# The lead panels of a stage take turns as the blocks of X come, the panel steps around the squares' sums are dealt out anew, and ScalarE writes two output blocks of each norm

## The reference

```python
h = _layer_norm(DEEPNORM_ALPHA * h + mix, ln_g[layer, 0], ln_b[layer, 0])
h = _layer_norm(DEEPNORM_ALPHA * h + _sq_relu_mlp(h, ffn_w1[layer], ffn_w2[layer]), ...)
# _layer_norm: mu = mean(x); var = mean((x - mu)^2); (x - mu) * rsqrt(var + eps) * g + b
```

## Time and profile before

| | us |
|---|---|
| median of 3 runs | 2793.14 |
| the profiled execution | 2793.86 |
| its span, first to last instruction | 2792.1 |
| PE busy | 2707.3 |
| DVE, ACT, POOL busy | 1281.0, 1016.3, 283.2 |
| mean granted clock of TensorE | 0.987 |

### The profile page before, as it was taken

The page is one execution under the profiler, slowest core; times in us unless marked ns, Lnnn a source line. Parts: engine busy times, 40 slices in busy tenths (PEclk is TensorE's granted clock), DMA queues, the critical chain, the costliest instruction groups (busy, mean ns, idle before and its releaser), DMA issues.

```text
span 2792.1 us, 39535 instructions
## 1 busy us (share of the span) xinstructions
PE 2707.3 (97%) x16362; PEld 2360.0 (85%) x16362; DVE 1281.0 (46%) x2178; ACT 1016.3 (36%) x1630; POOL 283.2 (10%) x357
## 2 busy tenths in 40 slices
PE   8999999999999999999999999999999999999997
PEld 7888899999988888788888888888888887888886
DVE  5544654334532323563334543435657655633333
ACT  4554443222322223352223432323567443522221
POOL 0000300001200000210000310002211121200003
PEclk9999999999999999999999999999999999999998
DMA  3111233222111212232222132222321212232220
GB/s 139 54 47 47 83 123 107 91 91 77 46 61 63 97 61 76 91 106 91 98 98 91 70 118 98 91 84 68 121 76 66 93 46 99 82 101 97 95 64 31
DMA packets 66531, 232.94 MB, mean 83 GB/s; under 512 B 8880, under 2 KB 9264, under 8 KB 65968
## 3 DMA queue, kind: packets, MB, share of 16 engines
q1 hardware_dynamic: 66352, 230.41, 24.8%
HBM read 228.25 MB, written 2.10 MB: 83 GB/s over the span
## 4 chain that ended last, share of the span: by engine, by line
PE 86%; DVE 5%; ACT 4%; POOL 2%; issue 2%; DMA 1%; SPq 0%; DVEq 0%; POOLq 0%; ACTq 0%
PE ps L578 75%; PE ps L887 2%; POOL R L2624 2%; PE ps L1013 1%; PE ps L588 1%; DVE R L1890 1%; PE ps L767 1%; PE ps L727 1%; DVE HT L1884 1%; ACT HT L1240 1%; POOL S L2610 1%; PE ps L874 1%; PE ps L598 1%; PE ps L1110 1%; PE ps L611 1%
## 5 line engine op out<-in xcount | busy, mean ns | idle before, releaser
L578 PE MATMUL ps<-XH,WH 128*128 128x264 f32 (+2 forms) x1856 | 538.3, 332 | 14.4 <-DVE XL L2584 8.6
L578 PE MATMUL ps<-XH,LENT 128*128 128x512 f32 (+2 forms) x2096 | 532.1, 343 | 8.0 <-DVE XL L1906 7.9
L578 PE MATMUL ps<-XL,WH 128*128 128x264 f32 (+2 forms) x1856 | 523.6, 324 | 0.0
L578 PE MATMUL ps<-XH,WL 128*128 128x264 f32 (+2 forms) x1856 | 522.7, 324 | 0.0
L578 PE MATMUL ps<-HH,LENT 128*128 128x264 f32 (+2 forms) x2220 | 491.1, 319 | 1.9 <-DVE LENT L1862 1.9
L1862 DVE TENSOR_TENSOR WL<-RAW,WH 128x1024 fp32r<-128x1024 f32 (+1 forms) x232 | 286.5, 1235 | 270.9 <-ACT WH L1210 270.6
L578 PEld LDWEIGHTS ps<-XH,LENT 128*128 128x128 f32 x2096 | 359.1, 190 | 60.0 <-DVE XL L1906 11.8
L578 PEld LDWEIGHTS ps<-HH,LENT 128*128 128x128 f32 x2220 | 361.4, 190 | 32.0 <-DVE LENT L1862 2.3
L578 PEld LDWEIGHTS ps<-XH,WH 128*128 128x128 f32 x1856 | 319.1, 189 | 56.7 <-issue 19.1
L578 PEld LDWEIGHTS ps<-XH,WL 128*128 128x128 f32 x1856 | 318.9, 189 | 28.1
L578 PEld LDWEIGHTS ps<-XL,WH 128*128 128x128 f32 x1856 | 319.1, 189 | 26.6
(11 more groups left out here) (215 smaller groups left out, 2625.1 us busy)
## 6 DMA issues: line engine op xcount, KB each, us to landing
RAW<-in_wf SPq DMA_DIRECT2D x128, 512.0 KB, 3.3
RAW<-in_wr SPq DMA_DIRECT2D x48, 512.0 KB, 3.3
RAW<-in_wg SPq DMA_DIRECT2D x44, 512.0 KB, 3.3
RAW<-in_wu SPq DMA_DIRECT2D x44, 512.0 KB, 3.3
RAW<-in_wd SPq DMA_DIRECT2D x32, 512.0 KB, 3.3
RAW<-in_we SPq DMA_DIRECT2D x24, 512.0 KB, 3.3
RAW<-in_wm SPq DMA_DIRECT2D x24, 512.0 KB, 3.3
RAW<-in_wro SPq DMA_DIRECT2D x16, 512.0 KB, 3.3
```

The lines of the kernel that those rows point to most:

```text
L578: mm = e.matmul(o[:, to:to + m], wt, xt[:, k, c0 + a * m:c0 + (a + 1) * m], start=(n == 0 and j == 0), stop=(n == nk - 1 and j == 2))
```

## The change

- `lead_turns` gives the order in which the lead panels take their steps. Half 0: five steps of panel 0, five of panel 1, three of each, then one panel after the other; for ln00 panels 0 to 2 by turns, with panels 3 and 4 put in. Half 1: panels 0 to 2 by turns for the eight blocks, then panel 3, then panel 4. An eviction follows its panel's eighth step. All three engines use the same order.
- `first_steps`: 12 instead of 8 steps ahead of the second total in ln00. Ahead of the squares' sums 20 instead of 17 steps, but for ln1 and mem.
- The output blocks k = 2 and 5 of every norm (not mem's) are written by ACT instead of POOL, from the same tile, behind XH of the same block; who reads them waits for `S.r_act`.
- `even`: three steps of weo 1 ahead of the turns of unit 41, two between them and the values, two behind, instead of seven ahead.
- `retention`: behind the first four steps of each of wro 8 to 10, four half-width steps each of wro 11 and wro 12 (`begun`); on ACT and DVE these stand behind `ret_out(3)`. ln10's ends split fewer panels ahead from the third one on (`ah.quiet`).

```diff
     def first_steps(ln, half):
-        return (6, 16 if ln == "ln1" else 8)[half]
+        return (6, {"ln1": 16, "ln00": 12}.get(ln, 8))[half]
+    def lead_turns(ln, half):
+        n = len(LEADS[ln])
+        if half == 1:
+            return [0, 1, 2] * 8 + [p for p in range(3, n) for k in range(8)]
+        if ln == "ln00":
+            return [0, 1, 2] * 7 + [0] + [3] * 6 + [1] + [3] * 2 + [4] * 4 + [2] + [4] * 4
+        return [0] * 5 + [1] * 5 + [0] * 3 + [1] * 3 + [p for p in range(2, n) for k in range(8)]
+    ACT_OUT = (2, 5)
+    def out_mark(ln, half, k):
+        return (S.r_act if ln != "mem" and k in ACT_OUT else S.r_out), (ln, half, k)
     def sums_at(name, idx, half):
...
             o = bank(("total", ln, half), 1, (S.mean, ln, half))
             w.wait_ge(*mark)
             e.matmul(o[:, 0:T], ONE[:, :], sums, start=True, stop=True).then_inc(*S.total(ln, half))
-            pump(17)
+            pump(17 if ln in ("ln1", "mem") else 20)
             rstd((ln, half), [(HT[:, 1, 0:T], S.add_pool[(ln, half, 4)]), (HT[:, 2, 0:T], S.add_dve[(ln, half, 7)])],
                  T, (S.normed, ln, half, 7), pump, 3)
...
                     freed = (S.q_copy, "crs", i, half)
                 else:
                     freed = (S.silu if name[1] == "g" else S.up, i, half)
-                yield gemm(name, idx, X, x_ready(ln, half), c0 + half * T // 2, T // 2, freed, half)
-        def down_norm(ln, done=0, midway=None, other=None, order=range(8)):
+                gens.append(gemm(name, idx, X, x_ready(ln, half), c0 + half * T // 2, T // 2, freed, half))
+            left = [8] * len(gens)
+            for p in lead_turns(ln, half) if gens else ():
+                next(gens[p])
+                left[p] -= 1
+                if not left[p]:
+                    drain(gens[p])
+                yield
+        def down_norm(ln, done=0, midway=None, other=None, order=range(8), begun=()):
...
-            leads = list(lead_pass(ln, 1))
-            for k in range(8):
-                for g in leads:
-                    next(g)
-            for g in leads:
-                drain(g)
+            drain(lead_pass(ln, 1))
...
                 next(ends[0])
             even_turn_v(7)
             even_back(40, pump)
-            for k in range(7):
-                next(ends[1])
+            pump = pumping(ends[1])
+            pump(3)
             even_back(41, pump)
+            pump(2)
             drain(ends[0])
             drain(ends[1])
             down_norm("ln00", 2)
...
                 if h == 1:
                     down("wro", 0, "ret0", NM, 512)
             ends = [down_block("wro", 8 + m, "ret1", NM, 512) for m in range(3)]
-            for n in range(12):
+            begun = [down_block("wro", 8 + m, "ret1", NM, 256, 0) for m in (3, 4)]
+            for n in range(20):
                 if n == 4:
                     ret_stat(3)
                 if n == 6:
                     ret_spread(3)
-                next(ends[n // 4])
+                next((ends + begun)[n // 4])
             for g in ends:
                 drain(g)
-            down_norm("ln10", 3)
+            down_norm("ln10", 3, begun=begun)
         def swiglu(n, ln_in, ln, midway=None, other=None):
...
@@ -1228,6 +1250,8 @@
             w.wait_ge(*S.total[ln, half])
             if normed[0]:
                 w.wait_ge(*S.r_out[normed[0]])
+                if normed[0][0] != "mem":
+                    w.wait_ge(*S.r_act[(*normed[0][:2], ACT_OUT[-1])])
             e.activation(HT[:, 0, 0:T], acc(("total", ln, half), 1)[:, 0:T], ACT.Copy, scale=inv).then_inc(*S.mean(ln, half))
             w.wait_ge(*S.const["eps"])
             e.activation(WARM, eps[LN_EPS], ACT.Sqrt)
...
                     w.wait_ge(*S.panel[final(AT[X_LAST[ln]])])
                     e.activation(XH[:, k, c:c + T], HT[:, T_SLOT[k], 0:T], ACT.Identity, bias=pcol(ln + "b", k),
                                  scale=pcol(ln + "g", k)).then_inc(*S.x_hi(ln, half, k))
+                if ln != "mem" and k in ACT_OUT:
+                    w.wait_ge(*S.normed[ln, half, k])
+                    e.activation(res(k), HT[:, T_SLOT[k], 0:T], ACT.Identity, bias=pcol(ln + "b", k),
+                                 scale=pcol(ln + "g", k)).then_inc(*S.r_act(ln, half, k))
                 pump(3)
             normed[0] = (ln, half, 7)
...
                 gate_up(name, idx, c, T, half)
         def lead_pass(ln, half):
-            for name, idx in LEADS[ln]:
-                yield from ah.steps(name, idx, half)
-                lead_evict(ln, name, idx, half)
-                if half == 1:
-                    ah.ahead(ah.panel)
-        def down_norm(ln, done=0, midway=None, other=None, dst=True, meanwhile=None):
+            gens = [ah.steps(name, idx, half) for name, idx in LEADS[ln]]
+            left = [8] * len(gens)
+            for p in lead_turns(ln, half) if gens else ():
+                next(gens[p])
+                yield
+                left[p] -= 1
+                if not left[p]:
+                    lead_evict(ln, *LEADS[ln][p], half)
...
             if midway:
                 midway(pumping(g))
             drain(g)
-            for nm, idx in ENDS[ln]:
-                drain(ah.steps(nm, idx, 0))
+            for n, (nm, idx) in enumerate(ENDS[ln]):
+                ah.quiet = ln == "ln10" and n > 1
+                drain(begun[n] if n < len(begun) else ah.steps(nm, idx, 0))
             ah.upto(ah.panel + (len(LEADS[ln]) or 2))
             ah.quiet = True
...
             def lower(k):
                 w.wait_ge(*S.x_hi[ln, half, k])
-                w.wait_ge(*S.r_out[ln, half, k])
+                sig, event = out_mark(ln, half, k)
+                w.wait_ge(*sig[event])
                 e.tensor_tensor(XL[:, k, c:c + T], res(k), XH[:, k, c:c + T].bitcast(F32),
                                 ALU.subtract).then_inc(*S.x_lo(ln, half, k))
             for k in range(9):
...
                 sums(*m)
             w.wait_ge(*S.par_in["par"])
             for k in range(8):
-                w.wait_ge(*S.normed[ln, half, k])
-                e.tensor_scalar(res(k), HT[:, T_SLOT[k], 0:T], pcol(ln + "g", k), pcol(ln + "b", k), ALU.mult,
-                                ALU.add).then_inc(*S.r_out(ln, half, k))
+                if out_mark(ln, half, k)[0] is S.r_out:
+                    w.wait_ge(*S.normed[ln, half, k])
+                    e.tensor_scalar(res(k), HT[:, T_SLOT[k], 0:T], pcol(ln + "g", k), pcol(ln + "b", k), ALU.mult,
+                                    ALU.add).then_inc(*S.r_out(ln, half, k))
                 for m in between.get(k, ()):
                     sums(*m)
```

More of the change, by code:

```diff
@@ L677, in down_norm @@
                     drain(fill)
-                    fill = other() if other else in_turn(lead_pass(ln, 0))
+                    fill = other() if other else lead_pass(ln, 0)
                 c = c0 + half * T // 2
@@ L1308, in lead_pass, with down_norm @@
         def lead_pass(ln, half):
[L1309 to L1315 removed]
+            gens = [ah.steps(name, idx, half) for name, idx in LEADS[ln]]
[6 more added lines that the diff above has]
+                    lead_evict(ln, *LEADS[ln][p], half)
+                    if half == 1:
+                        ah.ahead(ah.panel)
+        def down_norm(ln, done=0, midway=None, other=None, dst=True, meanwhile=None, begun=()):
             name, base, _, stage = end_of(ln)
@@ L1550, in retention @@
             ends = [ah.steps("wro", 8 + m) for m in range(3)]
+            begun = [ah.steps("wro", 8 + m, 0) for m in (3, 4)]
             for n in range(12):
@@ L1555, in retention @@
             ret_out(3)
+            for n in range(8):
+                next(begun[n // 4])
             for g in ends:
                 drain(g)
-            down_norm("ln10", 3)
+            down_norm("ln10", 3, begun=begun)
         def swiglu(n, ln, midway=None, other=None, dst=True, meanwhile=None):
@@ L2756, in sync @@
             for half in (0, 1):
-                w.wait_ge(*S.r_out["ln4", half, k])
+                sig, event = out_mark("ln4", half, k)
+                w.wait_ge(*sig[event])
             e.dma_start(out[:, k, :], R[:, k, NM:TW]).then_inc(*S.out_done(k))
```

17 lines of the change are left out of this document (9 added, 8 removed).

## The result

The changed kernel takes 2800.87 us (median of 15 runs, 2799.51 to 2802.45), the kernel before 2794.13 us on the same chip: a ratio of 1.0024 [1.0016, 1.0031], 6.7 us slower. The prediction was 2797.5. The profiled execution has a span of 2799.2 us, 7.1 more than before. PE's busy time is 1.5 us less than before, so in these two traces the loss shows as time in which PE stands, 8.6 us more of it.

A forecast was written before the change was run, and what follows sets the result against it. TensorE was busy 2707.3 of 2792.1 us, so only its idle time, low clock and tail could move. Gains of -9.4, losses of +9.6 and clock +4.2 gave +4.4: 2797.5 us, own range 2791 to 2804 (8 in 10: 2784 to 2807).

The forecast's parts named there:

- step 8: Second passes of four norms: new waits bring low-clock stretches, 0.6 per pass, costing +4.2 us (0 to 7).
- Step 1: Tail of the even mixer: waits of 0.94 and 1.45 us both go, -2.4 us.
- Step 6: Front of ln10: early panels stall 6.9 us for lent splits, +5.0, clock +1.7; turns win 2.6 back; second mean +0.7.
- Step 7: Five-lead second passes: sixteen steps left for the end; ln10 +5.5 us, ln11 +2.1, ln3 +1.6, ln00 +0.2.
- Step 5: Output blocks on ScalarE: 0.6 us per write, mostly hidden by idle time elsewhere; ln1 +0.2 us.
- Steps 2 and 3: Norms ln01 and ln2: mean about 1.9 us earlier, waits of 1.67 and 0.74 go; -2.6 and -2.0 us.
- Step 4: ln4, the end: fewer GpSimd outputs shorten the tail by 1.1 us and the mean comes earlier; -2.4 us.
- rival C: Behind ln10's stall and in five-lead passes: the low clock decides, 13.6 us in place of 4.2; 2807, chance 0.12.
- Rivals A and B: A: five-lead blocks keep pace with three steps, 2783, chance 0.18; B: ln10's early panels do not stall, about 2790, 0.13.

The follow-up runs named there:

- experiment 2: Changed kernel with retention's end as before (wro 11 and 12 not begun early, no quiet end in ln10); 2796.97 us, 1.0013 to the kernel before.
- experiment 1: Changed kernel with all leads taking one step per block in the second pass, as before; 2791.53 us, 0.9993 to the kernel before.
- experiment 10: As experiment 9, with GpSimd's last sum placed behind output block 5, not 6; 2783.51 us, 0.9969 to the kernel before.
- experiment 5: Changed kernel with all eight output blocks of every norm on GpSimd again; 2792.69 us, 0.9999 to the kernel before.
- experiment 6: Changed kernel with second pass's leads all in turn, retention's end as before, and seventeen steps ahead of the squares' sums everywhere; 2787.82 us, 0.998.
- 12: As experiment 9, with seventeen steps ahead of the squares' sums everywhere in place of twenty; 2782.64 us, 0.9961 to the kernel before.
- experiment 9: Changed kernel with second pass's leads all in turn, retention's end as before, and ScalarE's output writes in ln4 alone; 2779.75 us, 0.9953.
- Experiment 11: As experiment 9, with first-pass panels one after the other and eight steps ahead of ln00's second total; 2793.26 us, 1.0006 to the kernel before.

## Why the prediction was right, and where it was not

The size and the sign held (+4.4 forecast, +6.7 measured), but partly by luck: two errors cancelled, and the forecast's +4.4 was nearly all step 8, since the rows without the clock came to +0.2. The most likely class by the prediction's own chances, a time that can't be told from no change (0.42, up to 2798.7 us), is not what came.

Step 1 (-2.4): shown alone, -2.3, with both waits gone; its interval reaches zero.

Step 6: right in kind and size. The stall was 6.76 us for 6.9 forecast; undoing it gives 3.1 us, less than the 5.0 + 1.7 that the step names, since a wait at the total comes back in exchange (2.16 us in experiment 2; 2.91 in the earlier trace rows), as it said. Its own three terms make +3.8 for the first total, not the +3.2 of its 1176.2; measured from the end of ln01's leads it is +4.2. The turns then won 1.4 us back between ln10's two totals, not 2.6.

Step 7: the mechanism is right, and in ln10 the size too: +3.5 forecast for block 5 with 25 steps in place of 15, 3.6 us given back by experiment 1. For ln11, ln3 and ln00 the step names only net figures (2.1, 1.6, 0.2), with the first pass's gain inside; the net rows came out near (2.5, 2.1, -0.3), while undoing the order of three gives 3.2, 3.3 and 2.3 there and 8.7 us over all norms. In experiment 1 the granted clock around ln10 is 0.97 again, around ln00 0.98.

Step 5 is the one that failed. It took ScalarE's idle time as cover ("elsewhere ScalarE's idle time of 0.2 to 0.5 us hides most"). ScalarE did have the time; the order of two jobs whose results VectorE needs together was what cost. It had priced +0.6 to +1.1 for ln10 and +0.2 for ln1; the runs give 7 us for the whole kernel, about 8 with the gain at the end set against it. On the other side the first pass's turns are worth 14.8 us where the steps had some 2 us for each norm, about 11 together (1.9, 1.9, 2.6, 1.3, 2.1, and 1.3 for ln3). The two misses stood against each other.

Steps 2 and 3: the waits that they named did go (1.67 and 0.74), and ln2 still lost 0.9 us. Both said that the mean comes 1.9 us earlier because ScalarE and GpSimd are free by then. This step failed: the table of totals shows 0.2 us in ln01 and 0.8 in ln2. What is late next is the total itself: it waits 0.80 us for GpSimd's last sum, which hangs on VectorE's residual (experiment 10). The Trainium skill (Perfetto Trace Analysis, Optimizing Scalar/DVE Operations) says that moving work to another engine may pay where VectorE is saturated. That is another case than this one: here work went from GpSimd to ScalarE while VectorE set the pace of the norm, it took nothing off VectorE, and it cost 7.0 us (experiment 5). Behind the spread one step is left, and the first block is waited for 1.45 and 1.29 us, as forecast.

Step 4: -2.1 for -2.4, but not for its reasons. VectorE's eight products start and GpSimd's outputs end 1.0 us closer, as forecast (3.25 us for six). The span gets nothing of it. This row of the kernel before answers to the last one of after:
```profile
2784.98 4.32 SPq L2758 DMA_DIRECT2D out<-R  x8
```
SP needs 0.54 us to issue each of the eight output DMAs, starts 1.2 us behind the first product in both kernels, and ends 2.8 us before the span does in both. What was gained lies ahead: 1.5 us between ln4's two totals (16.24 before, 14.72 after) and 0.5 between total and mean. The three steps are not its cause once ScalarE writes: with seventeen steps and ScalarE's writes the totals stand 14.70 (experiment 6) and 14.72 us apart (12); with twenty and GpSimd's writes 15.25 (5).

Step 8: +4.2 is of the right order, but no run shows it as a cost. What the windows miss of full clock grew by 2 us in ln00, 5 to 6 in ln10, and not in ln11 and ln3; over the whole trace by some 5 us. Part of it lies under waits, in ln10 nearly all: one low stretch there falls on the 6.76 us stall and the other ends ahead of block 5 (experiment 1). In experiment 9 the stretch around ln00 has the full clock:
```profile
1140.00:1240.00 100.00, 93.20 (x634) 85.09 (x633) 71.42 (x122) 51.59 (x88) 25.83 (x33) 0.98 0.36 118
300.00:400.00 100.00, 93.06 (x760) 91.92 (x759) 62.21 (x113) 45.48 (x82) 20.14 (x27) 1.00 0.27 92
```
Of rival C (2807) only ln10 bears a trace, with two low stretches; in ln11 and ln3 there is one, as there was before. Rivals A and B are out: blocks did not come every 1.1 us between evictions, and the early panels did stall.

Open: what the three steps ahead of the squares' sums cost while the panels run one after the other. Experiment 11 has them beside the tail (-2.4) and ln4's writes (some -1), and gains nothing on the kernel before; with turns they can't be told from nothing (experiments 6 and 12), and no run has them alone. Why one order of the work draws more low clock than another is open too. The order of three in ln01 on top of experiment 9, whose leads still end in a 1.7 us wait, wasn't tried.

## What to carry to other kernels

Before giving an idle engine a piece of a chain, look at who consumes the piece and what else that engine makes for the same consumer: two results needed together belong on two engines. When panels share blocks that arrive slowly, let each block feed every panel as soon as it comes, since work that is kept for the end is paid in full. A multiplication pulled forward to fill a gap must have its weights there, not only its inputs.

## What was not expected of the hardware

- SP's issues of the output DMAs took 0.54 us each (4.31 to 4.32 for eight in every version). In the kernel before they can't be told from GpSimd's output blocks (4.30 for eight); in the kernel after GpSimd is done earlier, and the issues keep their pace and set that of the end.
- VectorE's XL took 0.42 us alone and 0.88 behind the start of GpSimd's sum of two blocks (1545.73 and 1545.87 in experiment 9). Beside a GpSimd output block the one that started first kept its usual time: XL from 1548.08 took 0.42 and the output block from 1548.14 took 0.79 in place of 0.56; in experiment 3 the output block from 1554.92 took 0.56 and XL from 1555.09 took 0.65. The Trainium skill (SBUF — State Buffer, SBUF: two separate sides) describes a port pair that VectorE and GpSimd lock for a whole instruction, also for a VectorE operation with two inputs in SBUF, and says that the one that starts first gets it. These rows agree.
- ScalarE's write of a 128x256 block with scale and bias takes 0.60 us, its plain copy 0.38, and two in a row start 0.50 apart.
